# Preparing the next expert's rows earlier in the trip of a mixture-of-experts loop

## Chip, cores and metric

The kernel runs on one core of a Trainium2 chip. The metric is the device time of one execution in microseconds (us). TensorE is called PE in the profile, its weight loads PEld, VectorE is DVE, ScalarE is ACT, GpSimd is POOL and SyncE is SP.

## What is computed

One inference step of a two-layer decoder on 256 prompt tokens and 32 sample tokens, 288 in all, with a model width of 1024. Layer 0 is a convolution module and a dense SwiGLU; layer 1 is sliding-window attention and a mixture of experts. The change is in the mixture alone:

```python
def moe_swiglu(x, g, w_router, w_eg, w_eu, w_ed):
    h = rms_norm(x, g)
    hf = h.reshape(-1, D_MODEL)
    logits = (hf @ w_router).astype(jnp.float32)
    top_v, top_i = lax.top_k(logits, TOP_K)          # 2 of 8
    gates = jax.nn.softmax(top_v, axis=-1)
    combine = jnp.einsum('tk,tke->te', gates, jax.nn.one_hot(top_i, N_EXPERTS))
    y = jnp.zeros_like(hf)
    for e in range(N_EXPERTS):
        he = jax.nn.silu(hf @ w_eg[e]) * (hf @ w_eu[e])   # 1024 -> 3584
        y = y + combine[:, e:e + 1] * (he @ w_ed[e])      # 3584 -> 1024
    return x + y.reshape(x.shape)
```

All is float32.

## The kernel before

Float32 products are made of three matmuls each: operands are split into a high part (`hi`, a rounding to fp32r) and a rest (`lo`, the value minus `hi`), and `mm3` (L331 to L335) adds hi x hi, hi x lo and lo x hi. ScalarE makes the high parts of the weights (L1013 `w_hi`, L1016 `d_hi`). VectorE makes the rest of the gate and up weights (L1394 `w_lo`, two units of 128 x 2048 a chunk), GpSimd that of the down weights (L1632 `d_lo`, one unit a chunk).

The experts are worked through in trips, one expert each: a trip takes the at most 128 tokens of its expert as 128 slots. There are eight trips in this run. A trip has 14 chunks of 256 hidden columns. TensorE's order in chunk ch (L739 to L761) is: the first half of gate and up of chunk ch + 1, the turn of `he` of chunk ch (two transposes, L718), the second half of gate and up of ch + 1, the down matmuls of ch (12 matmuls into banks 2 and 3), and in chunks 1 to 8 one `back`: it scatters one of eight column blocks of the previous expert's result to its tokens through the matrix PT, into bank 7, and VectorE adds it to X (L1484, `add_back`). Every engine runs its own program in order and waits on semaphores; nothing is reordered by a planner.

Weights come in units of 1 MB through SyncE's queue into six landing buffers; a unit is requested when the buffer's last content has been split (`split`, `d_split`).

Work for the next expert, in order:

- `turn_picks` (L678): TensorE transposes this trip's one-hot `pick` into bank 7 in chunk 10 (`GATES_AT`), after a wait for the last add-back; ScalarE copies it to PT in chunk 11 (L1067).
- `place` (L1450): VectorE writes the next expert's gates (`tok`) and its one-hot `pick`, three instructions, in chunk 11, between `he` and `heT_lo`.
- `slot_rows` (L672): TensorE multiplies `pick` with `tok` into two columns of bank 7, row number and gate of each slot, at the end of chunk 11.
- `slot_row_of` (L1458): VectorE writes the row numbers `slot_row` at the end of chunk 12, behind the two `w_lo` of that chunk.
- `gather_rows` (L1635): GpSimd issues the indirect DMA that fetches 128 rows of 4 KB into `xt`. It stands in GpSimd's program behind the `d_lo` of chunk 13, which GpSimd makes during chunk 12.
- `gather` (L666): TensorE transposes `xt` in chunk 13 into banks 4 and 5, ScalarE (L1057) and VectorE (L1478) split it into `xe_hi` and `xe_lo`. Half of it stands ahead of the turn of chunk 13, half behind, and the down matmuls of chunk 13 after both.
- At the end of the trip VectorE copies the gates of the slots from bank 7 to `slot_gate` (L1528), after the result of this expert has been scaled with the old ones.

Of the kernel before, what the change touches and what calls it, by code (L numbers as in the profile page):

```python
# [39 lines left out]
P = 128  # L40
D = 1024
KT_D = D // P
# [20 lines left out]
PASSES = -(-T // SLOTS)  # L63
GATES_AT = KT_D + 2
NOT_HERE = 4096.0
# [44 lines left out]
def build(nc, io):  # L110
    with ExitStack() as ctx:
# [27 lines left out]
        def phase(*tensors):  # L139
            phases[0] += 1  # L140
            with ExitStack() as stack:
# [32 lines left out]
               ("PT", [SLOTS, T], F32R), ("tok", [P, 3, 2], F32), ("slot_row", [SLOTS, 1], I32),  # L174
               ("slot_gate", [SLOTS, 1], F32), ("slot_of", [P, 3, PASSES * NE + 1], F32),
               ("gate_of", [P, 3, PASSES * NE + 1], F32), ("lg", [P, 6, 3, NE], F32), ("rt", [P, 3], F32),
               ("cmp", [P, 2, 3, NE, NE], F32), ("top", [P, 16], F32), ("trips", [1, 2], I32)]
        (d_hi0, d_hi1, d_lo0, d_lo1, oe_hi, oe_lo, pick, PT, tok, slot_row, slot_gate, slot_of, gate_of, lg, rt,
         cmp_, top, trips, xe_hi, xe_lo, xt, silu_g, he, heT_hi, heT_lo) = phase(
# [10 lines left out]
        def c(name):  # L190
# [45 lines left out]
                             "sel_ready", "pos_done", "route_ready"))  # L236
        h_stored, rt_inverse, htok_scaled, rows_placed, rows_ready, gates_ready, xt_ready, oe_hi_ready, zero_made, pick_zero, zero_stored, rows_seen = (
            sem(n) for n in ("h_stored", "rt_inverse", "htok_scaled", "rows_placed", "rows_ready", "gates_ready",
                             "xt_ready", "oe_hi_ready", "zero_made", "pick_zero",
                             "zero_stored", "rows_seen"))  # L240
        P_ready, gathered, xe_hi_ready, xe_ready, PT_done, PT_ready = (
# [88 lines left out]
        def _(pe):  # L330
# [341 lines left out]
            def slot_rows(out):  # L672

                for j, (t0, nt) in enumerate(TT):
                    last = pe.matmul(out[:, 0:2], pick[0:nt, j, :], tok[0:nt, j, :], start=(j == 0), stop=(j == 2))
                last.then_inc(rows_placed, 1)

            def turn_picks():  # L678

                for j, (t0, nt) in enumerate(TT):  # L680
                    last = pe.transpose(bank[7][:, t0:t0 + nt], pick[0:nt, j, :], ident[0:nt, 0:nt])
                last.then_inc(PT_done, 1)
# [20 lines left out]
            with pe.Fori(0, n_trips) as trip:  # L703
# [34 lines left out]
                for ch in range(NCH):  # L738
                    if ch + 1 < NCH:  # L739
                        gate_up(ch + 1, 0)  # L740
                        turn(ch)
                        gate_up(ch + 1, 1)
                    else:

                        with pe.If(trip < n_trips - 1):
                            gather(trip + 1, 0)
                        turn(ch)
                        with pe.If(trip < n_trips - 1):
                            gather(trip + 1, 1)
                    down(ch)  # L750
                    if 1 <= ch <= KT_D:
                        back(trip, ch - 1)
                    if ch == GATES_AT:
                        pe.wait_ge(y_added, trip * KT_D + KT_D)
                        turn_picks()
                    if ch == GATES_AT + 1:
                        with pe.If(trip < n_trips - 1):
                            pe.wait_ge(P_ready, trip + 2)
                            pe.wait_ge(PT_ready, trip + 2)
                            slot_rows(bank[7])  # L760
            for k in range(KT_D):  # L761
# [4 lines left out]
        def _(act):  # L766
# [294 lines left out]
            with act.Fori(0, n_trips) as trip:  # L1061
                for ch in range(NCH):
                    act.wait_ge(used, trip * (2 * NCH) + DENSE + 2 * ch + 2)
                    act.activation(silu_g[:], bank[ch % 2][:, 0:CH], ACT.Silu).then_inc(esilu_ready, 1)
                    if ch == GATES_AT + 1:
                        act.wait_ge(PT_done, trip + 1)
                        act.copy(PT[:, :], bank[7][:, 0:T]).then_inc(PT_ready, 1)  # L1067
                    if 2 <= ch + 1 < NCH:
# [31 lines left out]
        def _(dve):  # L1100
# [357 lines left out]
            def slot_row_of(n, src):  # L1458

                dve.wait_ge(rows_placed, n)  # L1460
                dve.tensor_scalar(slot_row[:], src[:, 0:1], -1.0, float(T), ALU.mult, ALU.add).then_inc(rows_ready, 1)

            place(0)
            slot_row_of(1, bank[0])
            dve.tensor_copy(slot_gate[:], bank[0][:, 1:2]).then_inc(gates_ready, 1)

# [22 lines left out]
            with dve.Fori(0, n_trips) as trip:  # L1489
                for ch in range(NCH):  # L1490
                    dve.wait_ge(esilu_ready, trip * NCH + ch + 1)
                    dve.tensor_tensor(he[:], silu_g[:], bank[ch % 2][:, CH:2 * CH], ALU.mult).then_inc(he_ready, 1)
                    if ch == GATES_AT + 1:
                        with dve.If(trip < n_trips - 1):
# [20 lines left out]
                    if 1 <= ch <= KT_D:  # L1515
                        add_back(trip, ch - 1)
                    if ch == GATES_AT + 2:
                        with dve.If(trip < n_trips - 1):
                            slot_row_of(trip + 2, bank[7])

# [5 lines left out]
                with dve.If(trip < n_trips - 1):  # L1526
                    dve.wait_ge(oe_ready, trip * 2 + 4)
                    dve.tensor_copy(slot_gate[:], bank[7][:, 1:2]).then_inc(gates_ready, 1)  # L1528
            for k in range(KT_D):
# [259 lines left out]
```

## Time and profile before

| | |
|---|---|
| median of 3 runs | 1745.76 us (1744.1 to 1746.47) |
| the profiled execution | 1742.29 us |
| its span | 1740.5 us |
| mean granted TensorE clock | 0.936 |
| busy PE, PEld | 1564.0 us, 1300.2 us |
| busy DVE, ACT, POOL | 1172.8 us, 959.6 us, 685.4 us |
| DMA | 431.39 MB, mean 248 GB/s |
| first and last fetch of a boundary | 743.68 us and 1589.68 us from the start |

A busy share is an average over stages. What the end of a stage waits for is read from the waits and from the timeline. In the rows, an idle time in brackets is that of the engine just before the instruction, with what ended it. Matmuls are pipelined: the length shown of one overlaps the next, and the distance between two starts is what one costs.

### The profile page before, as it was taken

The page shows a single profiled execution, that of the slowest core. Times are in us where ns is not written, and L with a number is a line of the kernel's source. Part 1 is how long each engine was busy: PE and PEld are TensorE (multiplying, and loading weights), DVE is VectorE, ACT ScalarE, POOL GpSimd, SP SyncE. Part 2 cuts the span into 40 slices and gives each one's busy share as a digit, 9 for nine tenths or more (in the row PEclk, how much of TensorE's full clock was granted, in tenths as well). Part 3 has the DMA queues.
Part 4 walks back from the last instruction along what each step waited for, and adds up shares of the span by engine and source line. Part 5 has one row for each costly group of instructions (what it writes and reads, how often), then busy time and mean ns, then how long its engine had stood idle before and what let it go on. Part 6 is the DMA issues. An engine that isn't in the chain of part 4 may idle for free.

```text
span 1740.5 us, 22307 instructions
## 1 busy us (share of the span) xinstructions
PE 1564.0 (90%) x7880; PEld 1300.2 (75%) x7880; DVE 1172.8 (67%) x1165; ACT 959.6 (55%) x999; POOL 685.4 (39%) x247
## 2 busy tenths in 40 slices
PE   6775999999978789979979979979997997997998
PEld 5764899999856668767767757757876876775786
DVE  5998545457774457767757766766775775776675
ACT  5412443345452447656656756647665765665664
POOL 5560111012210235545535535535544553553553
PEclk8888999999977789989989989999998998998999
DMA  8821244445340169969969969987986996995993
GB/s 312 158 85 53 78 161 162 162 143 193 125 175 25 67 248 353 340 254 351 348 235 355 356 231 348 353 323 265 353 334 255 351 346 246 342 353 229 360 354 131
DMA packets 64322, 431.39 MB, mean 248 GB/s; under 512 B 7861, under 2 KB 10165, under 8 KB 13712
## 3 DMA queue, kind: packets, MB, share of 16 engines
q1 hardware_dynamic: 57312, 412.38, 63.3%
q0 software_dynamic: 3616, 12.28, 3.0%
q10 hardware_dynamic: 3344, 6.05, 1.0%
q8 instruction: 32, 0.52, 0.1%
q14 instruction: 18, 0.15, 0.0%
HBM read 422.55 MB, written 9.14 MB: 248 GB/s over the span
## 4 chain that ended last, share of the span: by engine, by line
PE 72%; DVE 13%; issue 6%; ACT 4%; DMA 3%; POOL 1%; DVEq 0%; ACTq 0%; POOLq 0%
PE bank L333 22%; PE bank L335 21%; PE bank L334 21%; DMA xt<-h_rows,slot_row 3%; DVE C L1173 2%; DVE odd L1173 2%; ACT w_hi L1013 2%; DVE w_lo L1394 2%; DVE w_lo L1118 2%; PE bank L718 1%; PE bank L355 1%; DVE pick L1454 1%; PE bank L589 1%; PE bank L700 1%; PE bank L701 1%
## 5 line engine op out<-in xcount | busy, mean ns | idle before, releaser
L1632 POOL TENSOR_TENSOR d_lo<-land,d_hi 128x2048 fp32r<-128x2048 f32 x112 | 537.8, 4804 | 540.1 <-ACT d_hi L1016 540.1
L1394 DVE TENSOR_TENSOR w_lo<-land,w_hi 128x2048 fp32r<-128x2048 f32 x224 | 617.9, 2794 | 157.7 <-ACT w_hi L1013 156.7
L1013 ACT CAST w_hi<-land 128x2048 fp32r<-128x2048 f32 x224 | 417.2, 1910 | 3.5 <-issue 3.5
L333 PE MATMUL bank<-w_hi,xe_hi 128*128 128x512 f32 x896 | 367.9, 411 | 7.0 <-DVE xe_lo L1478 6.6
L335 PE MATMUL bank<-w_hi,xe_lo 128*128 128x512 f32 x896 | 355.5, 397 | 0.0
L334 PE MATMUL bank<-w_lo,xe_hi 128*128 128x512 f32 x896 | 355.1, 396 | 0.0
L1016 ACT CAST d_hi<-land 128x2048 fp32r<-128x2048 f32 x112 | 214.1, 1913 | 129.2 <-PE bank L335 129.2
L333 PEld LDWEIGHTS bank<-w_hi,xe_hi 128*128 128x128 f32 x896 | 169.4, 189 | 45.3 <-DVE w_lo L1394 12.9
L335 PEld LDWEIGHTS bank<-w_hi,xe_lo 128*128 128x128 f32 x896 | 169.1, 189 | 40.7
L333 PE MATMUL bank<-d_hi,heT_hi 128*128 128x512 f32 x448 | 184.7, 412 | 15.8 <-DVE heT_lo L1501 15.8
L334 PEld LDWEIGHTS bank<-w_lo,xe_hi 128*128 128x128 f32 x896 | 169.8, 189 | 32.3
L334 PE MATMUL bank<-d_lo,heT_hi 128*128 128x512 f32 x448 | 182.1, 406 | 0.0
L335 PE MATMUL bank<-d_hi,heT_lo 128*128 128x512 f32 x448 | 182.0, 406 | 0.0
L1118 DVE TENSOR_TENSOR w_lo<-land,w_hi 128x2048 fp32r<-128x2048 f32 (+1 forms) x56 | 132.2, 2367 | 31.9 <-ACT w_hi L781 31.5
L1075 ACT CAST heT_hi<-bank 128x256 fp32r<-128x256 f32 x112 | 41.7, 373 | 159.9 <-PE bank L718 159.9
L1501 DVE TENSOR_TENSOR heT_lo<-bank,heT_hi 128x256 fp32r<-128x256 f32 x112 | 47.4, 423 | 121.2 <-ACT heT_hi L1075 121.2
L333 PE MATMUL bank<-G_hi,w_hi 128*128 128x288 f32 x416 | 124.7, 300 | 0.3 <-PE bank L335 0.3
L334 PE MATMUL bank<-G_lo,w_hi 128*128 128x288 f32 x416 | 122.7, 295 | 0.0
L335 PE MATMUL bank<-G_hi,w_lo 128*128 128x288 f32 x416 | 122.3, 294 | 0.0
L333 PEld LDWEIGHTS bank<-d_hi,heT_hi 128*128 128x128 f32 x448 | 87.6, 195 | 42.4 <-POOL d_lo L1632 14.0
L781 ACT CAST w_hi<-land 128x2048 fp32r<-128x2048 f32 (+1 forms) x56 | 104.3, 1870 | 23.6 <-PE bank L335 22.2
L333 PE MATMUL bank<-H_hi,w_hi 128*128 128x288 f32 x272 | 88.0, 323 | 26.4 <-POOL H_lo L1539 13.5
(243 smaller groups left out, 2292.6 us busy)
## 6 DMA issues: line engine op xcount, KB each, us to landing
land<-in_w_expert SPq DMA_DIRECT2D x336, 1024.0 KB, 5.9
land<-in_w_dense SPq DMA_DIRECT2D x54, 1024.0 KB, 4.8
rel_rows<-rb POOLq DMA_DIRECT2D x1, 3072.0 KB, 37.9
bias<-rel_rows ACTq DMA_DIRECT2D x4, 512.0 KB, 5.4
X<-in_x SPq DMA_DIRECT2D x4, 288.0 KB, 6.1
out_y<-X SPq DMA_DIRECT2D x2, 576.0 KB, 3.3
Us<-in_state POOLq DMA_DIRECT2D x1, 1088.0 KB, 9.5
out_conv_s<-Us POOLq DMA_DIRECT2D x1, 1088.0 KB, 6.4
```

The source lines that it names most:

```text
L333: pe.matmul(out, w[0], x[0], start=start, stop=False)
L334: pe.matmul(out, w[0], x[1], start=False, stop=False)
L335: return pe.matmul(out, w[1], x[0], start=False, stop=stop)
L781: act.copy(w_hi[n % RING][:, 0:cols], land[n % LAND][:, 0:cols]).then_inc(hi_done, 1)
L1013: act.copy(w_hi[n % RING][:], land[(DENSE + u) % LAND][:]).then_inc(hi_done, 1)
L1016: act.copy(d_hi[ch % 2][:], land[(DENSE + u) % LAND][:]).then_inc(d_hi_done, 1)
L1075: act.copy(heT_hi[:], bank[6][:, 0:CH]).then_inc(heT_hi_ready, 1)
L1118: dve.tensor_tensor(w_lo[n % RING][:, 0:cols], land[n % LAND][:, 0:cols], w_hi[n % RING][:, 0:cols].bitcast(F32), ALU.subtract).then_inc(s ...
L1173: ins = dve.scalar_tensor_tensor(out=acc, in0=x, scalar=w_dw[:, j, w:w + 1], in1=acc, op0=ALU.mult, op1=ALU.add)
L1394: dve.tensor_tensor(w_lo[n % RING][:], land[slot][:], w_hi[n % RING][:].bitcast(F32), ALU.subtract).then_inc(split, 1)
L1501: dve.tensor_tensor(heT_lo[:], bank[6][:, 0:CH], heT_hi[:].bitcast(F32), ALU.subtract).then_inc(heT_ready, 1)
L1632: pool.tensor_tensor(d_lo[ch % 2][:], land[slot][:], d_hi[ch % 2][:].bitcast(F32), ALU.subtract).then_inc(d_split, 1)
```

## The change

The one-hot of the next expert, its slot rows and its row numbers are made in chunks 3 to 7 instead of 10 to 12. `turn_picks` writes bank 4 in chunk 3 and `slot_rows` bank 5 in chunk 6; both banks are otherwise used only by `gather`. `place` is in chunk 4. PT may not be overwritten before the last `back`, so ScalarE copies it in chunk 10, and `gather` waits for that copy before it writes bank 4. The gates, which bank 7 kept until the end of the trip, are copied to a new tile `next_gate` in chunk 7 and from there to `slot_gate` at the end. GpSimd's program is not changed.

```diff
-GATES_AT = KT_D + 2
+TURN_AT = 3
+SCATTER_AT = KT_D + 2
...
             def turn_picks():
 
                 for j, (t0, nt) in enumerate(TT):
-                    last = pe.transpose(bank[7][:, t0:t0 + nt], pick[0:nt, j, :], ident[0:nt, 0:nt])
+                    last = pe.transpose(bank[4][:, t0:t0 + nt], pick[0:nt, j, :], ident[0:nt, 0:nt])
                 last.then_inc(PT_done, 1)
...
                         with pe.If(trip < n_trips - 1):
+                            pe.wait_ge(PT_ready, trip + 2)
                             gather(trip + 1, 0)
...
-                    if ch == GATES_AT:
-                        pe.wait_ge(y_added, trip * KT_D + KT_D)
+                    if ch == TURN_AT:
                         turn_picks()
-                    if ch == GATES_AT + 1:
+                    if ch == TURN_AT + 3:
                         with pe.If(trip < n_trips - 1):
                             pe.wait_ge(P_ready, trip + 2)
-                            pe.wait_ge(PT_ready, trip + 2)
-                            slot_rows(bank[7])
+                            slot_rows(bank[5])
...
-                    if ch == GATES_AT + 1:
+                    if ch == SCATTER_AT:
                         act.wait_ge(PT_done, trip + 1)
-                        act.copy(PT[:, :], bank[7][:, 0:T]).then_inc(PT_ready, 1)
+                        act.wait_ge(y_done, trip * KT_D + KT_D)
+                        act.copy(PT[:, :], bank[4][:, 0:T]).then_inc(PT_ready, 1)
...
                 dve.wait_ge(rows_placed, n)
+                dve.tensor_copy(next_gate[:], src[:, 1:2]).then_inc(gate_kept, 1)
                 dve.tensor_scalar(slot_row[:], src[:, 0:1], -1.0, float(T), ALU.mult, ALU.add).then_inc(rows_ready, 1)
...
-                    if ch == GATES_AT + 1:
+                    if ch == TURN_AT + 1:
                         with dve.If(trip < n_trips - 1):
                             dve.wait_ge(PT_done, trip + 1)
                             place(trip + 1)
...
-                    if ch == GATES_AT + 2:
+                    if ch == TURN_AT + 4:
                         with dve.If(trip < n_trips - 1):
-                            slot_row_of(trip + 2, bank[7])
+                            slot_row_of(trip + 2, bank[5])
...
                     dve.wait_ge(oe_ready, trip * 2 + 4)
-                    dve.tensor_copy(slot_gate[:], bank[7][:, 1:2]).then_inc(gates_ready, 1)
+                    dve.wait_ge(gate_kept, trip + 2)
+                    dve.tensor_copy(slot_gate[:], next_gate[:]).then_inc(gates_ready, 1)
```

## Rows read from the trace of the kernel before

**Rows 1.** Page, part 1: engine, busy us, share of the span, instructions.

```profile
PE 1564.0 (90%) x7880; PEld 1300.2 (75%) x7880; DVE 1172.8 (67%) x1165; ACT 959.6 (55%) x999; POOL 685.4 (39%) x247
```

**Rows 2.** Table of waits: total us, times, longest.

```profile
PE bank L669 <- DMA xt<-h_rows,slot_row: 70.0, 8, 9.7
...
POOL xt L1639 <- DVE slot_row L1461: 43.1, 8, 6.5
```

**Rows 3.** The fetch by its line, landing; timeline, ahead of the first trip.

```profile
DMA to landing us min/median/max: 4.3/6.8/7.2
...
606.07 1.94 PE L669 MATMUL bank<-con,xt 128*128 128x128 f32 x8 [5.59 <-DMA xt<-h_rows,slot_row]
```

**Rows 4.** Timeline at the first boundary: start, us, engine, line [idle before].

```profile
737.90 4.89 DVE L1394 TENSOR_TENSOR w_lo<-land,w_hi 128x2048 fp32r<-128x2048 f32 x2 [1.38 <-ACT w_hi L1013]
...
738.30 0.40 PE L333 MATMUL bank<-d_hi,heT_hi 128*128 128x512 f32 x1
...
742.72 0.15 DVE L1461 TENSOR_SCALAR slot_row<-bank 128x1 int32<-128x1 f32 x1
...
743.68 0.98 POOL L1639 DMA_INDIRECT xt<-h_rows,slot_row  x1 [5.24 <-DVE slot_row L1461]
...
749.72 1.11 PE L669 MATMUL bank<-con,xt 128*128 128x128 f32 x4 [8.46 <-DMA xt<-h_rows,slot_row]
...
752.64 0.79 PE L333 MATMUL bank<-d_hi,heT_hi 128*128 128x512 f32 x1 [0.53 <-DVE heT_lo L1501]
```

**Rows 5.** Timeline of GpSimd, the d_lo of chunks 11, 12 and 13.

```profile
713.95 4.63 POOL L1632 TENSOR_TENSOR d_lo<-land,d_hi 128x2048 fp32r<-128x2048 f32 x1 [4.27 <-ACT d_hi L1016]
723.48 4.71 POOL L1632 TENSOR_TENSOR d_lo<-land,d_hi 128x2048 fp32r<-128x2048 f32 x1 [4.90 <-ACT d_hi L1016]
733.82 4.63 POOL L1632 TENSOR_TENSOR d_lo<-land,d_hi 128x2048 fp32r<-128x2048 f32 x1 [5.63 <-ACT d_hi L1016]
```

**Rows 6.** Timeline of an ordinary chunk, the seventh of the first trip.

```profile
687.24 0.44 DVE L1484 TENSOR_TENSOR X<-bank,X 128x288 f32<-128x288 f32 x1
687.24 4.64 POOL L1632 TENSOR_TENSOR d_lo<-land,d_hi 128x2048 fp32r<-128x2048 f32 x1 [4.28 <-ACT d_hi L1016]
...
687.60 0.40 DVE L1492 TENSOR_TENSOR he<-silu_g,bank 128x256 f32<-128x256 f32 x1
...
691.13 0.40 PE L333 MATMUL bank<-d_hi,heT_hi 128*128 128x512 f32 x1
```

**Rows 7.** Timeline: the one-hot ahead of the first trip, and in chunk 11.

```profile
598.24 0.66 DVE L1454 TENSOR_SCALAR pick<-con,slot_of 128x128 f32<-128x128 f32 x3
...
723.25 5.02 DVE L1454 TENSOR_SCALAR pick<-con,slot_of 128x128 f32<-128x128 f32 x3
...
728.20 0.41 DVE L1501 TENSOR_TENSOR heT_lo<-bank,heT_hi 128x256 fp32r<-128x256 f32 x1
...
728.54 4.47 DVE L1394 TENSOR_TENSOR w_lo<-land,w_hi 128x2048 fp32r<-128x2048 f32 x2
...
728.74 0.49 PE L333 MATMUL bank<-d_hi,heT_hi 128*128 128x512 f32 x1 [1.57 <-DVE heT_lo L1501]
```

**Rows 8.** DMA queues, 745.5 to 747.5 and 495 to 499: packets, MB, share.

```profile
q1 hardware_dynamic: 106, 0.87, 104.5%
...
q0 software_dynamic: 113, 0.95, 56.4%
```

**Rows 9.** Timeline at the end of the first trip: d_lo pair, gate copy.

```profile
756.41 11.58 POOL L1632 TENSOR_TENSOR d_lo<-land,d_hi 128x2048 fp32r<-128x2048 f32 x2 [11.75 <-ACT d_hi L1016]
...
764.87 0.16 DVE L1528 COPY slot_gate<-bank 128x1 f32<-128x1 f32 x1
```

**Rows 10.** Windows: stretch, length, busy PE, PEld, DVE, ACT, POOL, clock, DMA share, GB/s.

```profile
743.50:757.10 13.60, 6.85 (x21) 5.53 (x22) 4.01 (x4) 5.83 (x6) 1.67 (x2) 0.50 0.40 166
```

**Rows 11.** Timeline of the convolution's end: VectorE beside a GpSimd DMA.

```profile
133.06 0.47 DVE L1173 SCALAR_TENSOR_TENSOR C<-Up,w_dw,C 128x256 f32<-128x256 f32 x1
...
133.25 0.62 POOL L1592 DMA_DIRECT2D out_conv_s<-Us  x1
```

More of the change, by code:

```diff
@@ L174, in build @@
                ("PT", [SLOTS, T], F32R), ("tok", [P, 3, 2], F32), ("slot_row", [SLOTS, 1], I32),
-               ("slot_gate", [SLOTS, 1], F32), ("slot_of", [P, 3, PASSES * NE + 1], F32),
+               ("slot_gate", [SLOTS, 1], F32), ("next_gate", [SLOTS, 1], F32), ("slot_of", [P, 3, PASSES * NE + 1], F32),
                ("gate_of", [P, 3, PASSES * NE + 1], F32), ("lg", [P, 6, 3, NE], F32), ("rt", [P, 3], F32),
                ("cmp", [P, 2, 3, NE, NE], F32), ("top", [P, 16], F32), ("trips", [1, 2], I32)]
-        (d_hi0, d_hi1, d_lo0, d_lo1, oe_hi, oe_lo, pick, PT, tok, slot_row, slot_gate, slot_of, gate_of, lg, rt,
+        (d_hi0, d_hi1, d_lo0, d_lo1, oe_hi, oe_lo, pick, PT, tok, slot_row, slot_gate, next_gate, slot_of, gate_of, lg, rt,
          cmp_, top, trips, xe_hi, xe_lo, xt, silu_g, he, heT_hi, heT_lo) = phase(
@@ L236, in build @@
                              "sel_ready", "pos_done", "route_ready"))
-        h_stored, rt_inverse, htok_scaled, rows_placed, rows_ready, gates_ready, xt_ready, oe_hi_ready, zero_made, pick_zero, zero_stored, rows_seen = (
+        h_stored, rt_inverse, htok_scaled, rows_placed, rows_ready, gates_ready, xt_ready, oe_hi_ready, zero_made, pick_zero, zero_stored, rows_seen, gate_kept = (
             sem(n) for n in ("h_stored", "rt_inverse", "htok_scaled", "rows_placed", "rows_ready", "gates_ready",
                              "xt_ready", "oe_hi_ready", "zero_made", "pick_zero",
-                             "zero_stored", "rows_seen"))
+                             "zero_stored", "rows_seen", "gate_kept"))
         P_ready, gathered, xe_hi_ready, xe_ready, PT_done, PT_ready = (
@@ L674, in slot_rows @@
                 for j, (t0, nt) in enumerate(TT):
-                    last = pe.matmul(out[:, 0:2], pick[0:nt, j, :], tok[0:nt, j, :], start=(j == 0), stop=(j == 2))
+                    last = pe.matmul(out[:, 0:2], pick[0:nt, j, :], tok[0:nt, j, :],
+                                     start=(j == 0), stop=(j == 2))
                 last.then_inc(rows_placed, 1)
@@ L1464, in _ @@
             slot_row_of(1, bank[0])
-            dve.tensor_copy(slot_gate[:], bank[0][:, 1:2]).then_inc(gates_ready, 1)
+            dve.wait_ge(gate_kept, 1)
+            dve.tensor_copy(slot_gate[:], next_gate[:]).then_inc(gates_ready, 1)
             seq(dve.tensor_reduce(top[:, 8:9], STAT[:, 64:64 + NE], AX.X, ALU.max))
@@ L1527, in _ @@
                     dve.wait_ge(oe_ready, trip * 2 + 4)
-                    dve.tensor_copy(slot_gate[:], bank[7][:, 1:2]).then_inc(gates_ready, 1)
+                    dve.wait_ge(gate_kept, trip + 2)
+                    dve.tensor_copy(slot_gate[:], next_gate[:]).then_inc(gates_ready, 1)
             for k in range(KT_D):
```

## Prediction

> **What bounds the kernel now.** I read the shares of busy time first, then the table of waits, then the timeline at one boundary between two experts, then one ordinary chunk. TensorE is busy 90% of the span [rows 1], so only a stretch where it stands can give time back. In the table of waits the largest wait of TensorE inside the expert loop is for the gathered rows `xt`: 70.0 us in eight places [rows 2]. One of the eight, 5.59 us, is ahead of the first trip, where the fetch is not moved [rows 3]; the other seven are the boundaries, 70.0 - 5.6 = 64.4 us, 9.2 each.
>
> At the first boundary [rows 4] the down matmuls of chunk 12 start at 738.30 (I call this moment T). After them TensorE stands 8.46 us until `xt` lands and its transposes start at 749.72; the down matmuls of chunk 13 follow at 752.64. The fetch went out on GpSimd at 743.68, T + 5.38. What held it was `slot_row`, written at 742.72 to 742.87 behind two `w_lo` instructions of VectorE that began at 737.90. The table of waits says so too: GpSimd stood 43.1 us in eight fetches for `slot_row` [rows 2]. So at a boundary the end is set by VectorE's queue, then the fetch, then 2.92 us of turning and splitting.
>
> In an ordinary chunk [rows 5, 6] d_lo starts at 687.24 and again at 713.95 three chunks later, 8.90 us a chunk. There is little slack: `he` at 687.60 follows d_lo's start by 0.36, down starts at 691.13, 3.53 behind `he`, and d_lo ends at 691.88, 0.75 behind the start of down. The `w_lo` pair cannot start under d_lo, which shows best in the 5.02 us that three `pick` instructions take at 723.25 under a d_lo that starts at 723.48 and ends at 728.19 [rows 5, 7]; free of GpSimd the three take 0.66 [rows 7].
>
> **The change, part by part.** All sums are against the profiled execution, 1742.29 us with a span of 1740.5, which is 3.5 us under the median of 1745.76. I subtract from the median.
>
> *The fetch.* GpSimd's program is unchanged: the fetch still stands behind the d_lo of chunk 13 in its queue. With `slot_row` written in chunk 7 it leaves when that d_lo ends, not in chunk 7. Chunk 12 is then an ordinary chunk, so d_lo ends at T + 0.75 [rows 6]. From the end of `slot_row` to the fetch it took 743.68 - 742.87 = 0.81 us [rows 4]; behind a finished instruction of its own queue it may be near 0. I take 0.4, between the two: the fetch at T + 1.15 instead of T + 5.38, 4.2 us earlier (3.8 to 4.6). From issue to landing it takes 4.3 us at least, 6.8 at the median and 7.2 at most [rows 3]. The 4.3 is the fetch ahead of the first trip. In a boundary it waits behind weight units: from 745.5 to 747.5 the weight queue alone fills the DMA engines while the fetch is pending [rows 8]. In the new place it meets the units that are requested as d_lo(13) and the `w_lo` pair end, so I keep the same landing time, and allow 1 us less to 1.5 more. TensorE's wait falls from 9.2 to about 5.0 us. Nothing else is late next: `he` of chunk 13 is the instruction right behind `slot_row` on VectorE, which ended at T + 4.57 [rows 4], ahead of a landing at T + 8. Seven boundaries by 4.2: -29.4 us.
>
> *The one-hot.* Its `tok` copy and three `pick` instructions move from chunk 11 to chunk 4 and keep their place behind `he`. Before, the first two slip in ahead of d_lo and the third is held; heT_lo starts at 728.20 and TensorE stands 1.57 us [rows 7]. In chunk 4 no copy of PT delays d_hi, so d_lo is already running when `he` starts (0.36 ahead, rows 6). All of them wait until `he` + 4.28, then 0.66 for the group, 0.41 for heT_lo and 0.1 for the semaphore: down at `he` + 5.45, against 3.53 in an ordinary chunk, +1.9. Before, the stall was 1.57. The difference is 0.3 a trip, over 7 trips 2 us. VectorE's add-back, 0.44 us [rows 6], which chunk 4 has and chunk 11 has not, comes between the `w_lo` pair and the next `he`; TensorE needs that `he` only after its 12 down and 12 gate matmuls, so it is covered.
>
> *turn_picks and slot_rows.* The same three transposes and six small matmuls go from chunks 10 and 11 to 3 and 6. Before, the d_lo starts after them are 9.53 and 10.34 us apart instead of 8.90 [rows 5]; the excess is the turn, the PT copy and the stall together. In chunk 3 part of the turn now lies under the stall of chunk 4 (-0.3), and the PT copy in chunk 10 finds its transposes done, so ScalarE no longer stands for them (-0.3). `wait y_added` goes; the new waits (`y_done` at chunk 10, `PT_ready` ahead of the gather, `P_ready` at chunk 6) are for events chunks earlier. I put -0.4 a trip on this, eight trips, -3 us, bounds 0 and -6.
>
> *Two small copies.* `next_gate` from PSUM in chunk 7 costs some 0.1 us, covered by the delay that slot_rows gives TensorE one chunk ahead. The copy of `next_gate` to `slot_gate` takes the place of one from PSUM that needed 0.16 us while GpSimd was in a d_lo [rows 9]. What it costs from SBUF under GpSimd is not in the trace. The nearest rows are 0.16 and the held `pick`, some 4.6 us. I take 0.16, since it moves one element, and the other is a rival.
>
> *Clock.* The granted clock is 0.50, that is 1.2 GHz, from 743.5 to 757.1 [rows 10]: it had fallen some 2 us after TensorE went idle and rose 4.5 us after dense matmuls came back, which costs the down matmuls of chunk 13 about 2 us. TensorE would still stand 5 us and then run only sparse transposes for 2.9, so I keep this cost; the bound below is 7 x 2 = 14 us.
>
> Sum: -29.4 + 2 - 3 = -30.4, so some -30: 1745.8 - 30 = 1716.
>
> **The rivals.**
>
> *Held at the port (1731).* When d_lo(13) ends, a `w_lo` is already waiting, and it runs 2.2 us; the second follows. If GpSimd, to read `slot_row` and write descriptors, must wait for the first, the fetch leaves at T + 3.1 and saves 2.3 a boundary: -16, with the rest some -15. For it: the alternation of w_lo and d_lo. Against it: at 133.06 and 133.25 GpSimd's DMA instruction took 0.62 us beside VectorE instructions with two SBUF inputs [rows 11]; but that one reads no index. The Trainium skill (SBUF — State Buffer, Who interferes with whom) says that a VectorE instruction with two SBUF inputs contends with a GpSimd instruction that reads SBUF, and infers that descriptor writing needs another interface; by that rule this rival hangs on how the index is read, and the trace agrees only with its second half.
>
> *The copy to `slot_gate` is held (1735).* It comes at 764.87, under a d_lo that ends at 767.99 [rows 9]. Held till then, `he` of chunk 0 is 2.7 us late and TensorE stands for it: +19, giving -11. The Trainium skill (Advanced Engine Details and Errata, VectorE Performance Modes) gives the two-port mode only to even counts or equal odd counts above one, which a single element is not; no run here shows this, and by that rule the copy is free.
>
> *The queue hides it (1738).* If the fetch always waits until the weight queue is empty, three units end when they end now and it saves about 1 us a boundary: -8. For it: rows 8, first line. Against it: at 495 to 499 GpSimd's queue had 56% of the engines while a weight unit was being fetched [rows 8].
>
> *Clock kept (1702).* A shorter gap leaves 2.4 GHz granted in most boundaries.
>
> *Slower: the next `w_lo` meets the next d_lo (1756).* Behind the stall of chunk 11 the pair ran 728.54 to 733.01 and d_lo started at 733.82, a margin of 0.8 us [rows 5, 7]. Behind the stall of chunk 4 the same pair stands with less slack around it. If d_lo(6) comes first, it runs from `he` + 10.6 to 15.2 and the second `w_lo` ends at 17.5, where TensorE's gate_up wants it at 11.9: 5.6 us, and 7 x (5.6 - 4.2) = +10. It decides from 0.8 us of drift; I find 0.3.
>
> *Fetched in chunk 7 (1666).* Were the change what its title says, the whole 9.2 us and the clock would go, 11.4 x 7 = -80. GpSimd's order speaks against it.
>
> **How the numbers follow.** Chances: forecast 0.60, held at the port 0.13, held copy 0.09, queue 0.07, clock kept 0.05, slower 0.04, fetched early 0.02. The forecast's own range is 1707 to 1727. To hold 8 in 10 I take in port, copy and queue above and the clock below: 1702 to 1738. This kernel can tell 0.2%, 3.5 us. Within it fall the tail of the queue rival and a balance of two prices: 0.06; slower by more 0.05; faster 0.89.
>
> **What would show it.** Right: GpSimd's wait for `slot_row` gone in seven of eight fetches, each fetch directly behind a d_lo, TensorE's wait for `xt` near 40 us in all, `pick` some 5 us in chunk 4, fetch to landing still 6 to 8. Wrong: a fetch that starts behind a `w_lo`; a copy to `slot_gate` of several us; a landing over 9 us; a TensorE wait of several us in chunks 4 to 6 for `w_lo` or `he`.

## The result, and the profile after

The changed kernel takes 1735.0 us (median, 1734.2 to 1735.5) beside 1744.9 us for the kernel before, a ratio of 0.9942 (95% interval 0.9925 to 0.996). It is faster by 9.9 us. Forecast were 30 us: the sign and the place are right, the size is a third. The profiled execution took 1735.46 us with a span of 1733.6.

I read the same views in the same order. The page of the changed kernel, part 1, answers to [rows 1]; the table of waits to [rows 2]; the fetch by its line to [rows 3].

```profile
PE 1572.0 (91%) x7880; PEld 1305.6 (75%) x7880; DVE 1166.2 (67%) x1173; ACT 959.9 (55%) x999; POOL 697.0 (40%) x247
```

```profile
PE bank L670 <- DMA xt<-h_rows,slot_row: 61.0, 8, 8.4
...
POOL xt L1644 <- DVE slot_row L1464: 6.6, 1, 6.6
```

```profile
L1644 POOL DMA_INDIRECT xt<-h_rows,slot_row x8: 1087/2839/2854, 603.5 to 1580.6; - x8
...
DMA to landing us min/median/max: 4.2/9.9/10.4
```

GpSimd waits for `slot_row` once, ahead of the first trip, instead of eight times: the change does what its diff says. But TensorE's wait for `xt` fell only from 70.0 to 61.0 us, where about 40 was forecast. Two numbers of the third view say where the gain went. The fetch instruction (min, median and max in ns) takes 2839 ns, not the 957 of the kernel before, and from issue to landing 9.9 us pass instead of 6.8.

The first boundary in the timeline (start, us, engine, line, count, and in brackets the idle time ahead), as [rows 4]:

```profile
736.22 4.63 POOL L1637 TENSOR_TENSOR d_lo<-land,d_hi 128x2048 fp32r<-128x2048 f32 x1 [4.28 <-ACT d_hi L1017]
...
739.68 5.52 DVE L1396 TENSOR_TENSOR w_lo<-land,w_hi 128x2048 fp32r<-128x2048 f32 x2 [1.39 <-ACT w_hi L1014]
...
740.07 0.40 PE L334 MATMUL bank<-d_hi,heT_hi 128*128 128x512 f32 x1
...
741.00 2.85 POOL L1644 DMA_INDIRECT xt<-h_rows,slot_row  x1 [0.16 <-issue]
...
741.01 4.69 SPq L312 DMA_DIRECT2D land<-in_w_expert  x3
...
751.26 1.12 PE L670 MATMUL bank<-con,xt 128*128 128x128 f32 x4 [8.23 <-DMA xt<-h_rows,slot_row]
...
754.19 0.79 PE L334 MATMUL bank<-d_hi,heT_hi 128*128 128x512 f32 x1 [0.53 <-DVE heT_lo L1505]
```

T, the start of the down matmuls of chunk 12, is 740.07. The fetch starts at T + 0.93, 0.15 behind d_lo's end and 0.2 earlier than forecast. Its instruction then lasts until 743.85. VectorE's `w_lo` pair is recorded from 739.68, but d_lo ran until 740.85; the first of the two is recorded for 3.32 us instead of 2.3 and ended at 743.00. The fetch instruction got through 0.85 us later. The boundary in numbers, mean of the seven in each kernel, all counted from T. (The first boundary of the kernel before, which [rows 4] show, is the shortest of its seven: down of chunk 13 comes at 14.34 there, in the other six at 14.98 to 15.54. In the changed kernel all seven lie between 13.18 and 14.26.)

| | fetch starts | instruction | `xt` seen by TensorE | down of chunk 13 | from there to the next down |
|---|---|---|---|---|---|
| before | 5.38 | 0.96 | 12.16 | 15.09 | 16.45 |
| after | 0.92 | 2.84 | 10.88 | 13.81 | 16.68 |

So 4.46 us earlier at the issue became 1.28 us at `xt`: 1.88 went into the longer instruction and 1.3 into a longer way from its end to `xt` (5.8 before, 7.1 after). Over seven boundaries that is -8.9. The rest of the account: the stretch behind down of chunk 13 is 0.23 us longer (+1.6), the rest of a trip 0.07 shorter (-0.5), the last trip with the end of the program 0.9 shorter (-0.9), and this execution reached its first trip 1.9 us later, which no part of the change touches. Together -6.8, as much as lies between the two profiled executions.

Inside a trip the two stalls came where they were expected. The timeline of VectorE in chunk 4 answers to [rows 7]:

```profile
662.77 0.41 DVE L1496 TENSOR_TENSOR he<-silu_g,bank 128x256 f32<-128x256 f32 x1
663.10 3.92 DVE L1454 COPY tok<-gate_of 128x3 f32 x1
666.93 0.66 DVE L1456 TENSOR_SCALAR pick<-con,slot_of 128x128 f32<-128x128 f32 x3
667.52 0.40 DVE L1505 TENSOR_TENSOR heT_lo<-bank,heT_hi 128x256 fp32r<-128x256 f32 x1
```

### The profile page after: what moved, and what is told of

It reads as the page before. It is cut to its first block, busy times and chain, and to the rows that moved or that the text cites. A ratio compares the mean times of both kernels' runs of the same rounds, so it can differ in the third digit from the quotient of the medians.

```text
span 1733.6 us, 22322 instructions
## 1 busy us (share of the span) xinstructions
PE 1572.0 (91%) x7880; PEld 1305.6 (75%) x7880; DVE 1166.2 (67%) x1173; ACT 959.9 (55%) x999; POOL 697.0 (40%) x247
## 3 DMA queue, kind: packets, MB, share of 16 engines
q10 hardware_dynamic: 3344, 6.05, 1.0%
## 4 chain that ended last, share of the span: by engine, by line
issue 33%; PE 29%; POOL 24%; DVE 10%; ACT 1%; DMA 1%; POOLq 0%; ACTq 0%; DVEq 0%
POOL d_lo L1637 23%; PE bank L334 8%; PE bank L336 8%; PE bank L335 8%; DVE C L1175 2%; DVE odd L1175 2%; DVE w_lo L1120 2%; PE bank L356 1%; POOL xt L1644 1%; PE bank L590 1%; DMA xt<-h_rows,slot_row 1%; DVE C L1188 1%; ACT w_hi L782 0%; PE bank L579 0%; PE bank L549 0%
```

## Experiments

All but one start from the changed kernel; none leaves out work. Times are medians; each ratio stands to the kernel before on the same chip.

The theory after the first look: (1) the fetch is held at its issue by the `w_lo` pair; (2) its packets then share the DMA engines with the weight units. The rivals: the fetch takes no part in the gain at all; the 2.84 us are the queue's and not VectorE's; the landing is the fetch's own time.

### The fetch's place in the program

**The fetch alone, moved in the kernel before.**

```diff
                         with dve.If(trip < n_trips - 1):
+                            slot_row_of(trip + 2, bank[7])
                             expert_lo(trip, ch + 2, 0)
...
-                    if ch == GATES_AT + 2:
-                        with dve.If(trip < n_trips - 1):
-                            slot_row_of(trip + 2, bank[7])
```

> The kernel before with one edit: in chunk 12 VectorE computes slot_row ahead of its pair of w_lo subtractions instead of behind it; the one-hot, its turn and slot_rows stay in chunks 10 to 12. Theory (all of the change's gain comes from the earlier issue of the fetch, and that gain is cut by the hold of the fetch under the w_lo pair and by a longer landing): the fetch leaves within 1.2 us of down of chunk 12, its instruction takes 2.4 to 2.9 us instead of 0.96, xt lands 9.5 to 10.4 us after the issue, down of chunk 13 comes 13.3 to 14.0 us behind that of chunk 12 (15.1 in the kernel before), 1.1 to 1.8 us in each of 7 boundaries, 1732 to 1737 us. Rival (the gain is that of the moved one-hot and turn, and the earlier fetch brings nothing): 1743 to 1746 us. Second rival (the fetch is not held where GpSimd has waited for slot_row for a while): the instruction takes 0.96 us, xt lands 8 us after the issue or less, and the time is below 1725.

Measured: 1731.3 us, ratio 0.9917 (0.9903 to 0.993), just under the 1732 to 1737 expected. The fetch by its line, and in the timeline of GpSimd (T is 739.39):

```profile
L1637 POOL DMA_INDIRECT xt<-h_rows,slot_row x8: 1087/2838/2849, 602.7 to 1577.0; - x8
DMA to landing us min/median/max: 4.1/10.3/10.7
```

The fetch starts 0.3 us behind T, is held as long as in the changed kernel, and down of chunk 13 comes at 13.4. One moved line has all of the change's gain. By the medians it has 4 us more, but the two intervals touch (0.9930 and 0.9925); its boundaries are 0.37 us shorter than those of the changed kernel, 2.6 us in seven.

**All of the change but the fetch.** Both columns are kept in chunk 7, and `slot_row` is made in chunk 12 behind the `w_lo` pair.

```diff
-                dve.tensor_copy(next_gate[:], src[:, 1:2]).then_inc(gate_kept, 1)
-                dve.tensor_scalar(slot_row[:], src[:, 0:1], -1.0, float(T), ...
+                dve.tensor_copy(next_gate[:], src[:, 0:2]).then_inc(gate_kept, 1)
...
+                    if ch == SCATTER_AT + 2:
+                        with dve.If(trip < n_trips - 1):
+                            slot_row_out(trip + 2)
```

> The changed kernel without its earlier fetch: row and gate are copied from the PSUM bank in chunk 7 as in the change (both columns in one copy), but slot_row itself is computed in chunk 12 behind the w_lo pair, as in the kernel before. So everything of the change is in it except the fetch's time. Theory (the moves of the one-hot, the turn and slot_rows are worth 0.2 us a trip together, all else is the fetch): fetch 5.4 us behind down of chunk 12, instruction 0.96 us, landing 6.8 us, 1742 to 1745 us. Rival (the moves brought the change's gain, and the fetch nothing): 1733 to 1737 us.

Measured: 1751.4 us, ratio 1.0031 (1.002 to 1.0042): slower than the kernel before by 6.5 us. Neither theory had this. A trip's first twelve pitches (a pitch is the time from the start of one chunk's down matmuls to that of the next) add up as in the changed kernel (109.39 us against 109.45 before), so the moves themselves cost nothing there. At the boundary:

```profile
738.04 5.54 DVE L1396 TENSOR_TENSOR w_lo<-land,w_hi 128x2048 fp32r<-128x2048 f32 x2 [1.38 <-ACT w_hi L1014]
743.51 0.14 DVE L1468 TENSOR_SCALAR slot_row<-next_gate 128x1 int32<-128x1 f32 x1
...
744.47 0.98 POOL L1651 DMA_INDIRECT xt<-h_rows,slot_row  x1 [5.24 <-DVE slot_row L1468]
```

T is 738.43 here. In the kernel before, the stall in chunk 11 pushed TensorE's T back by 0.64 us against d_lo: d_lo ended at T + 0.15, the pair took 4.89 [rows 4], and the fetch left at T + 5.38. Without that stall d_lo ends at T + 0.78, the pair takes 5.54, and the fetch leaves at T + 6.01; down of chunk 13 comes at 16.44 instead of 15.09. A stall that was taken out of chunk 11 had been hiding part of the boundary's wait: 0.63 of the 1.35 us. The other 0.73 is a longer way from the issue to `xt` (7.51 instead of 6.78 in the mean), most of it in two of the seven boundaries, which land after 8.7 and 8.8 us and the other five after 6.8 to 7.3; why is open. Against this kernel the earlier fetch of the change is worth 16 us; against the kernel before it nets 10.

**The fetch in chunk 8.**

```diff
                     if 2 <= ch + 1 < NCH:
                         expert_lo(trip, ch + 1)
+                    if ch == TURN_AT + 5:
+                        with pool.If(trip < n_trips - 1):
+                            gather_rows(trip + 1)
                 with pool.If(trip < n_trips - 1):
-                    gather_rows(trip + 1)
                     expert_lo(trip, NCH)
```

> The changed kernel with one more edit: GpSimd issues the next expert's row fetch behind d_lo of chunk 9, in chunk 8, instead of behind that of chunk 13, in chunk 12. Theory (the boundary still costs what the fetch's arrival makes it cost, and the arrival is late because the fetch is held at its issue and then lands among the weight units): TensorE's wait for xt (61.0 us in 8) falls to that of the first trip alone, about 4 us; the first piece of the boundary then waits for he of chunk 13 only, and down of chunk 13 starts about 7 us behind that of chunk 12 instead of 13.8, so 6.8 us in each of 7 boundaries, 48 us: 1687 us; if the granted clock no longer drops at the boundaries, up to 2 us more in each: 1673. Rival one (something else, such as the PT copy or the xe split, ends the boundary at almost the same time as xt did): less than 15 us are gained, 1720 or more. Rival two (the fetch in the middle of a trip delays the weight stream there by what it saves at the boundary): the wait for xt is gone, but pitches of chunks 8 to 11 grow from 8.9 to 10 us or more, and the time is 1710 to 1730.

Measured: 1685.4 us, ratio 0.9657 (0.9642 to 0.9672). Down of chunk 13 comes at 7.1. In the timeline of the first boundary (T is 737.98) TensorE turns `xt` at once and then waits for `he`:

```profile
740.79 0.60 PE L670 MATMUL bank<-con,xt 128*128 128x128 f32 x4
...
743.50 0.44 PE L720 MATMUL bank<-con,he 128*128 128x128 f32 x2 [2.12 <-DVE he L1496]
```

The fetch instruction still takes 2.85 us there and lands 9.7 us after its issue; nobody waits for either, and the chunks around it keep their 8.9 us. The granted clock stays at 1.00 (2.4 GHz) at this boundary and at two others; at the other four it still falls to 0.50 (1.2 GHz), for 3.4 us, once for 6.8, where the changed kernel has 13.7 us of it at each of the seven. What that is worth can be read in a window from down of chunk 13 to the next down (length, busy PE, PEld, DVE, ACT, POOL, clock, DMA share, GB/s), first here, then in the changed kernel:

```profile
745.01:761.30 16.29, 14.53 (x62) 11.43 (x63) 10.93 (x9) 12.54 (x11) 11.49 (x2) 1.00 0.63 243
```

```profile
754.19:770.69 16.50, 16.50 (x62) 13.17 (x63) 10.95 (x9) 12.64 (x12) 11.58 (x2) 0.85 0.39 156
```

At 0.85 TensorE fills the whole stretch; at 1.00 it stands 1.8 us in it, waiting for `he` behind ScalarE and VectorE, and the stretch is 0.2 us shorter. Over all boundaries the stretch takes 16.24 to 16.29 us in this kernel where the clock stays, 16.66 to 16.69 where it falls, and 16.68 in the mean of the changed kernel. So the drop costs about 0.4 us a boundary in this stretch, 3 us in all.

**The fetch one chunk earlier than in the change**, ahead of the d_lo it stood behind.

> The changed kernel with the fetch one chunk earlier: issued by GpSimd ahead of d_lo of chunk 13, 8.1 us ahead of down of chunk 12, instead of behind it. Theory (held 2.84 us and landed 9.9 us after the issue as before, xt is there 1.8 us behind down of chunk 12, 1 us before TensorE comes to its transposes at 2.8): the wait for xt is gone as in the kernel with the fetch in chunk 8, 1685 to 1691 us. Rival (the unit packets ahead of the fetch, which run without a gap there, make the landing 11 us or more): TensorE still waits 0.5 to 2 us for xt in most boundaries, and the time is 1690 to 1700 us.

Measured: 1685.6 us, ratio 0.9658 (0.9642 to 0.9675). It leaves at T - 8.0 and lands a median of 10.2 us later, in time at five boundaries and 0.5 us late at two. One chunk is enough; the rival's longer landing is there (10.2, not 9.9), but down of chunk 13 comes at 7.03 at the two late boundaries too.

### Hold and traffic

**VectorE's `w_lo` pair behind the fetch.**

```diff
                     gather_rows(trip + 1)
+                    pool.memset(top[:, 15:16], 0.0).then_inc(fetch_out, 1)
                     expert_lo(trip, NCH)
...
                         with dve.If(trip < n_trips - 1):
+                            dve.wait_ge(fetch_out, trip + 1)
                             expert_lo(trip, ch + 2, 0)
```

> The changed kernel with one more wait: GpSimd sets a semaphore behind the fetch instruction, and VectorE's pair of w_lo subtractions in chunk 12 waits for it, so that no VectorE operation with two inputs in SBUF runs while the fetch is issued. Theory (the fetch instruction takes 2.84 us instead of 0.96 because VectorE's first w_lo subtraction holds it): the instruction takes 0.96 us again, xt comes about 1.9 us earlier in each of 7 boundaries, 13 us: 1722 us; the w_lo pair starts about 1 us later and ends under the wait for xt, which costs nothing; where the landing grows by what the issue gains, the gain is from 5 us on (1730). Rival (the 2.84 us are the DMA queue's, which is full of weight packets, and VectorE has no part in them): the instruction still takes 2.8 us, and the time is 1735 us or up to 7 us more.

Measured: 1707.8 us, ratio 0.9782 (0.9769 to 0.9796). The timeline (T is 738.31):

```profile
739.23 0.98 POOL L1645 DMA_INDIRECT xt<-h_rows,slot_row  x1
...
740.44 4.49 DVE L1396 TENSOR_TENSOR w_lo<-land,w_hi 128x2048 fp32r<-128x2048 f32 x2 [3.91 <-POOL top L1669]
```

The instruction is back at 0.98 us, so the hold is shown: VectorE's `w_lo` subtraction, which has two inputs in SBUF, makes it. But the gain is 27 us, twice the 13 expected: `xt` comes 3.74 earlier a boundary, twice the 1.9 of the hold.

**The next two weight units behind `xt`.** SyncE issues the unit that follows only when TensorE has seen `xt`.

```diff
-                        if j < 2:
+                        if u == LAND:
+                            sp.wait_ge(xt_seen, trip + 1)
+                        elif j < 2:
...
+            pe.wait_ge(split, DENSE + 1)
+            pe.sem_inc(xt_seen, 1)
...
                             pe.wait_ge(PT_ready, trip + 2)
+                            pe.wait_ge(xt_ready, 16 * (trip + 2))
+                            pe.wait_ge(split, trip * (2 * NCH) + (2 * NCH + DENSE + 1))
+                            pe.sem_inc(xt_seen, 1)
                             gather(trip + 1, 0)
```

> The changed kernel, but SyncE holds the weight units of the next trip that VectorE's w_lo pair sets free in chunk 12 (issued 3.1 and 5.3 us behind down of chunk 12) until TensorE has seen xt land. Theory (the landing is 9.9 us from the issue instead of 6.8 since, beyond the hold of 1.9 us, the fetch's packets share the DMA engines with one more unit of 512 KB): the landing, counted from the issue of the fetch, falls by 1.3 us at least, to 8.6 us or less, and by up to 3 us if both units were in its way; down of chunk 13 moves from 13.8 us behind that of chunk 12 to 12.5 or less, 9 us in 7 boundaries: 1726 us, down to 1715; the held units are needed two chunks later and arrive in time. Rival one (the landing is the time of the fetch's own 128 rows, whatever else is in the queues): landing 9.9 us, 1735 us. Rival two (the held units come too late): the landing falls but chunks 1 and 2 of the next trip grow by 1 us or more each, and the time is 1735 to 1750.

Measured: 1711.3 us, ratio 0.9809 (0.9795 to 0.9823). A unit is 1 MB, not the 512 KB of that text. The hold is still there (2.85 us), and yet `xt` is seen at 7.65 instead of 10.88, 3.2 us earlier where 1.3 to 3 were expected. The held units come in time: no pitch of the next trip changes.

**Both.**

> The changed kernel with both edits of the two runs before: VectorE's w_lo pair waits for the fetch instruction, and SyncE holds the next two weight units until TensorE has seen xt. The first alone gave 1707.8 us (xt lands 6.1 us after the issue), the second alone 1711.3 us (6.3 to 7.5 us). Theory (what costs is how many weight units stand in the DMA queue ahead of the fetch or beside it; the hold of 1.9 us costs mainly by letting one more unit in ahead; the two edits take away the same unit): the gains don't add, xt lands 5.8 to 6.3 us after the issue, down of chunk 13 comes 9.6 to 10.1 us behind that of chunk 12, 1703 to 1709 us. Rival (hold and traffic are two separate prices, 3.8 and 3.3 us a boundary, and add up): xt lands 3.5 to 4 us after the issue, down of chunk 13 at about 7.5, 1685 to 1690 us.

Measured: 1708.9 us, ratio 0.9787 (0.9773 to 0.98). The gains don't add: with no units behind it, taking the hold away as well changes `xt` from 7.65 to 7.47. So the hold has no price of its own worth naming. Its price is the weight unit that is issued 2.2 us after the first and gets ahead of the fetch while it is held.

**A third unit held**, beside both edits: the one issued at T + 0.94, just ahead of the fetch.

```diff
+                        elif u == LAND - 1:
+                            sp.wait_ge(xt_seen, trip + 1)
...
+                            pe.wait_ge(d_split, trip * NCH + (NCH + 2))
```

> The kernel with both edits (1708.9 us), in which SyncE holds a third weight unit until TensorE has seen xt: the one that GpSimd's last d_lo sets free and that was issued 0.94 us behind down of chunk 12, just ahead of the fetch (each unit is 1 MB; the 512 KB named for them in an expectation before was wrong). Theory (the fetch lands when the weight packets issued ahead of it have run, and its own part is small): with nothing new ahead of it, xt lands about 4.2 us after the issue, as in the first trip, down of chunk 13 comes 8.0 to 8.6 us behind that of chunk 12 instead of 10.2, 1.6 to 2.2 us in each of 7 boundaries: 1693 to 1698 us, and up to 3 us less if the granted clock no longer drops; if the three held units then come late for chunks 1 and 2 of the next trip, it shows as longer pitches there. Rival (the 6.2 us are the fetch's own, since 0.52 MB have to be gathered row by row, and the weight units have no part in them): landing 6.2 us, 1707 to 1710 us.

Measured: 1698.7 us, ratio 0.973 (0.9713 to 0.9746), just above the 1693 to 1698 expected, and the landing a median of 4.2 us after the issue, as ahead of the first trip [rows 3]. Of the 9.9 us from issue to landing, then, less than half is the fetch's own.

The trace has the packets of both queues. In the kernel with the `w_lo` pair behind the fetch, the fetch's instruction ends at 740.21. From 740 to 743.3 only the weight queue moves anything (packets, MB, share of 16 engines), and no packet of the fetch is there; then, from 743 to 745, all 144 of them are, with few of the weights:

```profile
q1 hardware_dynamic: 134, 1.06, 86.1%
```

```profile
q0 software_dynamic: 144, 0.52, 64.0%
q1 hardware_dynamic: 46, 0.25, 31.7%
```

In the changed kernel the fetch's packets are spread over 745 to 750, and the weight queue moves three times their bytes beside them:

```profile
q1 hardware_dynamic: 218, 1.52, 73.8%
q0 software_dynamic: 141, 0.52, 27.9%
```

With three units held, from 744 to 746, the fetch has the engines to itself:

```profile
q0 software_dynamic: 121, 0.43, 57.7%
```

From the fetch's issue until TensorE sees `xt`, 741.00 to 751.26 at the first boundary of the changed kernel, 3.42 MB of weights go through; the answer for the kernel before, over 743.68 to 749.72, stands behind it:

```profile
q1 hardware_dynamic: 465, 3.42, 83.0%
q0 software_dynamic: 144, 0.52, 13.7%
```

```profile
q1 hardware_dynamic: 240, 1.70, 67.7%
```

The table puts the boundary kernels side by side, means of seven boundaries from T. "Half" is the time from the end of the fetch instruction to the start of the middle one of its 144 packets, read from the packet records.

| | fetch | instr. | half | `xt` | down 13 | us |
|---|---|---|---|---|---|---|
| before | 5.38 | 0.96 | 4.3 | 12.16 | 15.09 | 1744.9 |
| all but the fetch | 6.01 | 0.96 | 4.5 | 13.51 | 16.44 | 1751.4 |
| after | 0.92 | 2.84 | 4.6 | 10.88 | 13.81 | 1735.0 |
| row first, in before | 0.30 | 2.84 | 4.7 | 10.51 | 13.44 | 1731.3 |
| two units held | 0.92 | 2.84 | 2.15 | 7.65 | 10.48 | 1711.3 |
| pair behind fetch | 0.92 | 0.96 | 4.0 | 7.14 | 10.07 | 1707.8 |
| both | 0.91 | 0.96 | 3.9 | 7.47 | 10.37 | 1708.9 |
| three units held | 0.92 | 0.96 | 1.9 | 5.58 | 8.76 | 1698.7 |
| ahead of the first trip | | 1.08 | 1.8 | | | |

The pattern shows when the middle packet is counted from T (the first three columns added up). It starts at 3.8 with no unit issued ahead of the fetch, at 5.8 to 5.9 with one, whether the fetch gets through at 1.9 or at 3.8, at 8.4 with two, and at 10.6 with three (the kernel before, whose units leave 0.6 earlier): some 2.5 us a unit. That is also why the hold is free with two units held: the one unit ahead runs out while the fetch is held.

The packet records say how. With one unit ahead the first packet of the fetch starts at T + 4.9 to 5.0, when that unit has nearly run, and the last ends 1.7 to 2.1 us later. In the changed kernel the first starts at T + 6.05, behind the first unit, but the last ends only 4.5 us later (means of seven): 1.2 MB of weights, about the second unit, which was issued 0.7 us before the fetch got through, move between them. So a unit that was issued well ahead of the fetch makes it wait, and one that was issued just ahead shares the engines with it. What the third unit alone costs, no run here shows.

### The one-hot

**Behind heT_lo instead of behind `he`, in chunk 4.**

```diff
-                    if ch == TURN_AT + 1:
-                        with dve.If(trip < n_trips - 1):
-                            dve.wait_ge(PT_done, trip + 1)
-                            place(trip + 1)
                     if ch == NCH - 1:
...
                                       ALU.subtract).then_inc(heT_ready, 1)
+                    if ch == TURN_AT + 1:
+                        with dve.If(trip < n_trips - 1):
+                            dve.wait_ge(PT_done, trip + 1)
+                            place(trip + 1)
```

> The changed kernel, but in chunk 4 VectorE makes the one-hot (tok copy and three picks) behind heT_lo instead of ahead of it. Theory (the 1.8 us by which the pitch from chunk 3 to chunk 4 is longer than an ordinary one are those of heT_lo, late behind a tok copy that d_lo holds for 3.9 us): heT_lo comes at its usual time, the tok copy is still held until the end of d_lo, the w_lo pair starts about 1.1 us late, and the pitch falls from 10.67 to between 8.9 and 9.7 us, 1.0 to 1.8 us in each of 7 trips: 1723 to 1728 us. Rival (TensorE needs the first w_lo as early as it needs heT_lo): the pitch stays at 10.5 or more, 1734 us or above.

Measured: 1727.0 us, ratio 0.9896 (0.9882 to 0.991). The `tok` copy is held 2.00 us, until the end of d_lo, and the pitch from chunk 3 to 4 falls from 10.67 to 9.48, that is 1.19 x 7 = 8.3 us. What stays over 8.9 is the three transposes of the turn: the last trip, which makes no one-hot, has 9.47 too.

**Fetch in chunk 8, and the one-hot between the two `w_lo` of chunk 4.**

```diff
...
                         expert_lo(trip, ch + 2, 0)
+                        if ch == TURN_AT + 1:
+                            with dve.If(trip < n_trips - 1):
+                                dve.wait_ge(PT_done, trip + 1)
+                                place(trip + 1)
                         expert_lo(trip, ch + 2, 1)
...
```

> The kernel with the fetch in chunk 8 (1685.4 us), and in chunk 4 VectorE makes the one-hot between the two w_lo subtractions, at a time when GpSimd has no d_lo to do, instead of behind he. Theory (tok copy and picks cost 0.7 to 0.8 us where no d_lo runs, and 4.6 us under one): the tok copy takes 0.2 us or less, nothing is held, the second w_lo ends 0.8 us later; the pitch from chunk 3 to 4 is 8.9 us, and that of 4 to 5 at most 9.8: 0.9 to 1.8 us less in each of 7 trips, 1672 to 1679 us. Rival (the copy is held there too, or the later second w_lo stalls TensorE by as much as heT_lo did): 1684 us or above.

Measured: 1675.6 us, ratio 0.96 (0.9586 to 0.9613), the fastest kernel here, 4% under the kernel before. In its timeline nothing is held:

```profile
667.40 0.15 DVE L1454 COPY tok<-gate_of 128x3 f32 x1
667.48 0.66 DVE L1456 TENSOR_SCALAR pick<-con,slot_of 128x128 f32<-128x128 f32 x3
```

The pitches are 9.47 and 8.97, not the 8.9 and up to 9.8 expected; the sum is right.

## Why the prediction was wrong, point by point

**What bounds the kernel: right.** The seven waits for `xt` were the place to gain. The kernels with an early fetch lose them, but for 0.5 us at two boundaries of one of them, and reach 1685 us. The reading that VectorE's queue set the fetch's start was right as well.

**The fetch, -29.4: wrong, measured -8.9.** The start was forecast at T + 1.15 and came at T + 0.92. The step that failed is "so I keep the same landing time, and allow 1 us less to 1.5 more". From the issue until TensorE sees `xt` it became 9.96 us on average instead of 6.78, 3.2 more: 1.88 in the instruction, 1.3 behind it. A landing over 9 us was the prediction's own sign of being wrong, and it came (9.9). The working treated 6.8 as a duration that moves with the fetch. Much of it was a queue: half of the fetch's packets had started 4.3 us behind the end of its instruction at a boundary, and 1.8 us behind it ahead of the first trip. I had the 4.3 us minimum landing and the full weight queue side by side [rows 3, 8], and should have asked when the units ahead of the fetch end in the new schedule. The units go by d_lo and by the `w_lo` pair, not by the fetch. Three are issued 0.94, 3.1 and 5.3 us behind T; before they left at 0.31, 2.46 and 4.66. A fetch that gets through at T + 3.8 has two units of some 2.5 us each ahead of it, where one that left at T + 1.15 with an instruction of 0.96 us would have had one.

**The rivals were priced as alternatives, and two came true together.** "Held at the port" (chance 0.13, 1731) named the hold exactly: the fetch gets through behind the first `w_lo`, 1.9 us later. What spoke against it was the DMA instruction of [rows 11], 0.62 us beside such VectorE instructions; the prediction itself said that this one reads no index, and still gave the rival only 0.13. Whether reading the index is what makes the difference, no run here shows. "The queue hides it" (0.07, 1738, 1 us a boundary) has nearly the right size, 1.28; its picture of an empty queue is too strict, since in the changed kernel the fetch's packets run among those of the second unit. Two of the experiments show that these are one mechanism: a fetch held 1.9 us lets a unit pass, and the unit costs more than the hold. The Trainium skill (SBUF — State Buffer, Who interferes with whom) also says that a DMA which seems stalled by a VectorE operation is one whose descriptors GpSimd writes, short of port time. The trace agrees: 2.84 us against 0.96. The prediction drew on that section's sentences about reading and about descriptor writing, which left the rival open, and not on this one.

**The stall as cover: not seen.** The forecast compared the two stalls of the one-hot (1.57 and 1.9) and put the difference at 2 us. It did not ask what the stall in chunk 11 covered. It stood one chunk ahead of the boundary and took 0.63 us of the boundary's wait with it. The kernel with all but the fetch shows it: 6.5 us above the kernel before, where up to 3 below was expected; 0.63 in each of seven boundaries is 4.4 us of the 9.4 by which its boundaries grew. The sum had counted this once already, without saying so, since it took T + 0.75 as the end of d_lo; it had not moved the weight units with it.

**The one-hot and the turn: right.** Forecast +0.3 and -0.4 a trip, so -0.1; the twelve pitches of a trip went from 109.45 to 109.38. In chunk 4 the group waited for d_lo's end and down came 10.67 behind the last, where 8.90 + 1.9 = 10.8 was forecast. That the copy and all three picks waited, not the third alone, is as written.

**Two small copies: right.** The copy from SBUF to `slot_gate` took 0.15 us under a d_lo pair that ran from 757.95 to 769.5:

```profile
766.48 0.15 DVE L1533 COPY slot_gate<-next_gate 128x1 f32<-128x1 f32 x1
```

The `tok` copy, three elements a partition, was held 3.92 us under a d_lo. The rival of 1735 us falls, although the time fell there. The rule of the Trainium skill (Advanced Engine Details and Errata, VectorE Performance Modes) that the prediction quoted holds in both cases.

**Clock: wrong in size, harmless.** The prediction kept the drop, and it stayed. But its price was put at 2 us a boundary, and the kernel with the fetch in chunk 8 shows 0.4 in the stretch behind the boundary, between its boundaries at 1.00 and those where the clock falls. The bound of 14 us below, and with it the rival of 1702, was several times too large: at 1.00 TensorE waits for `he`, behind ScalarE and VectorE.

**Slower, by `w_lo` meeting the next d_lo: didn't happen.** The pitches behind chunk 4 are 8.98 and 8.91.

**The range** of 1702 to 1738 held the time, at its far end, and that was partly luck: its edge came from the port and the queue taken one at a time, and nothing in it says what the two cost together.

## What to carry to other kernels

A landing time read from a trace is a queue's length as much as a transfer's duration: before moving a DMA, list which transfers are issued ahead of it in the new order and when they end, and look for an issue of the same transfer into an empty queue to see its own share. A transfer whose address is known early belongs a whole stage ahead of its use, where holds and queues cost nothing (chunk 8 or 11 here, 1685 us, 60 under the kernel before); moved only to the front of its own stage it may meet new neighbours. When a stall is removed, ask what it had been hiding.

## What the runs showed of the hardware

- An indirect DMA instruction on GpSimd takes 0.96 us free and 2.84 us when a VectorE `tensor_tensor` with both inputs in SBUF runs as it is issued, in all seven boundaries, and the same in the middle of a trip.
- Its packets don't start beside a weight unit that was issued well ahead of them: for 3.1 us after the end of its instruction none moved, at all seven boundaries of the kernel with the pair behind the fetch, while (at the first of them) the other queue had 86% of the engines. With nothing ahead the first started 0.7 us after the end of the instruction. The Trainium skill (DMA: Bandwidth & Descriptors, Queues, rings and completion order) says that each DMA engine takes turns between the queues that have work. The trace agrees for a unit issued just ahead of the fetch, whose 1.2 MB and the fetch's 0.52 MB run side by side for 4.5 us in the changed kernel; in the 3.1 us above it doesn't, and the measurement decides. Why the packets start late was not tried further.
- 128 rows of 4 KB land 4.2 us after the issue with no unit issued ahead, 6.1 with one, and 9.9 held and with two.
- A `tensor_copy` of one element a partition from SBUF is not held under GpSimd's subtraction (0.15 us); one of three elements is, until it ends (3.92 and 2.00 us).
